# An expert layer that adds its rows to x in memory, in place of a last stage that gathers them

## The reference

```
x = x + m                                   # m: the token mixers
h = rmsnorm(x, norm2_w)
p_grp = softmax(h @ w_router_g)             # 4 groups, the best one is taken
le_sel = (h @ w_router_e) of that group     # 4 experts in it
top_v, top_i = top_k(softmax(le_sel), 2);  top_v /= sum(top_v)
comb = one_hot(expert) * top_v * p_top      # 2 of 16 experts have a weight
act = silu(h @ w_gate[e]) * (h @ w_up[e]) * comb[e]
x = x + sum over e of act @ w_down[e]
y = rmsnorm(x, final_norm_w)
```

## Time and profile before

| | us |
|---|---|
| median of three runs | 1851.73 |
| the profiled execution, of which all rows below are | 1848.95 |
| its span, first to last instruction | 1847.1 |
| expert rounds, first gather wait to last store issue | about 1380 to 1781 |
| final stage, first load of x to the end | 1789.2 to 1847.1 |

### The profile page before, as it was taken

The page is one execution under the profiler, slowest core; times in us unless marked ns, Lnnn a source line. Parts: engine busy times, 40 slices in busy tenths (PEclk is TensorE's granted clock), DMA queues, the critical chain, the costliest instruction groups (busy, mean ns, idle before and its releaser), DMA issues. The chain is left out here.

```text
span 1847.1 us, 24874 instructions
## 1 busy us (share of the span) xinstructions
PE 1468.5 (80%) x8651; PEld 1301.3 (70%) x8651; DVE 1025.1 (55%) x1328; ACT 610.6 (33%) x918; POOL 343.7 (19%) x327
## 2 busy tenths in 40 slices
PE   3789999999997278878876956999928888798940
PEld 2789999999994277777766814888726667577730
DVE  4775455212222466666765146554158887788937
ACT  3332222211103023223322003333216665667723
POOL 0000001000000133242240000000002444344532
PEclk8899999999998589989987557999958998999975
DMA  2111122321112412112112044333146667653238
GB/s 119 53 45 46 35 81 82 113 90 55 65 36 111 136 26 45 30 25 50 25 25 111 1 155 154 119 104 103 49 171 227 231 229 270 251 207 113 92 139 321
DMA packets 91580, 200.53 MB, mean 109 GB/s; under 512 B 39227, under 2 KB 59963, under 8 KB 86655
## 3 DMA queue, kind: packets, MB, share of 16 engines
q1 hardware_dynamic: 74031, 135.48, 22.8%
q0 software_dynamic: 17488, 64.32, 9.6%
HBM read 205.96 MB, written 47.29 MB: 137 GB/s over the span
## 5 line engine op out<-in xcount | busy, mean ns | idle before, releaser
L87 DVE TENSOR_TENSOR c_wlo<-c_w,c_whi 128x1024 fp32r<-128x1024 f32 x40 | 49.0, 1226 | 262.7 <-ACT c_whi L82 262.4
L98 PE MATMUL c_ps<-hn_lo,c_whi 128*128 128x368 f32 x960 | 182.4, 332 | 7.0 <-DVE c_wlo L87 7.0
L98 PE MATMUL c_ps<-hn_hi,c_wlo 128*128 128x368 f32 x960 | 181.3, 331 | 0.0
L98 PE MATMUL c_ps<-hn_hi,c_whi 128*128 128x368 f32 x960 | 181.1, 331 | 0.0
L2244 DVE TENSOR_TENSOR e_winlo<-e_win,e_winhi 128x2048 fp32r<-128x2048 f32 x66 | 153.6, 2330 | 46.8 <-ACT e_winhi L2193 36.9
L98 PEld LDWEIGHTS c_ps<-hn_lo,c_whi 128*128 128x128 f32 x960 | 164.9, 189 | 7.3 <-DVE c_wlo L87 7.3
L98 PEld LDWEIGHTS c_ps<-hn_hi,c_wlo 128*128 128x128 f32 x960 | 164.3, 188 | 0.0
L98 PEld LDWEIGHTS c_ps<-hn_hi,c_whi 128*128 128x128 f32 x960 | 163.9, 188 | 0.0
L2193 ACT CAST e_winhi<-e_win 128x2048 fp32r x66 | 122.5, 1905 | 62.4 <-issue 42.4
L2107 POOL TENSOR_TENSOR e_wdnlo<-e_wdn,e_wdnhi 128x1024 fp32r<-128x1024 f32 x33 | 91.5, 2773 | 234.8 <-ACT e_wdnhi L2201 234.8
L82 ACT CAST c_whi<-c_w 128x1024 fp32r<-128x1024 f32 x40 | 42.1, 1052 | 224.7 <-PE c_ps L98 219.0
(11 more groups left out here) (466 smaller groups left out, 2978.9 us busy)
## 6 DMA issues: line engine op xcount, KB each, us to landing
e_win<-in_w_gate_up SPq DMA_DIRECT2D x33, 2048.0 KB
e_wdn<-in_w_down SPq DMA_DIRECT2D x33, 1024.0 KB
c_w<-in_w_in SPq DMA_DIRECT2D x40, 512.0 KB, 3.6
expert_rows<-e_ys POOLq DMA_DIRECT2D x33, 512.0 KB, 5.5
rc_eb<-g_rows SPq DMA_DIRECT2D x10, 624.0 KB, 5.3
o_land<-in_w_out SPq DMA_DIRECT2D x8, 768.0 KB, 4.9
rc_gb<-g_rows SPq DMA_DIRECT2D x11, 507.0 KB
n_x<-in_xT SPq DMA_DIRECT2D x2, 2208.0 KB, 10.2
```

The costliest lines, as they stand in the source:

```text
L87: return dve.tensor_tensor(dst, src, hi.bitcast(F32), ALU.subtract)
L98: mm = pe.matmul(dst, left(x, k), right(z, k), start=(n == 0 and k == 0), stop=(n == 2 and k == ks - 1))
```

## The change

The expert rows are no longer kept in a tensor of their own. Each round's rows are multiplied by their slot's weight while they are taken from PSUM (`slot_w`, one value for each of the 128 slots of the round), and POOL sends them by an indirect transfer with the operation add to the rows of `x2_dram` that `idx_out` names. An empty slot has the weight 0 and points to one of 128 spare rows behind the 1104, its own lane's; the spare rows are filled once, in the mixer output stage. Since a token has two rows in different rounds, a transfer may not start before the one of the round ahead has landed: POOL waits for `y_sent` of it. The routing stage makes `slot_w` and the occupancy of the slots with the same matmul as `idx_in`, 99 columns wide in place of 33. The last stage has no gathers and no weights: it loads x, takes the norm and stores.

```diff
--- before.py
+++ after.py
@@ -1587,9 +1587,11 @@
                 pool.dma_start(x2_dram[cols(t), :], x2[0:n]).then_inc(x2_sent, 16)
+                if t == 0:
+                    pool.dma_start(x2_dram[T:T + P, :], x2).then_inc(x2_sent, 16)
...
@@ -1906,7 +1909,7 @@
                 for i in range(k * NT9, (k + 1) * NT9):
-                    mm = pe.matmul(ps_idx[:, 0:NBLK], lo_hot[:, i, :], tok_hi[:, i, :], start=(i == 0), stop=(i == NK - 1))
+                    mm = pe.matmul(ps_idx[:, 0:3 * NBLK], lo_hot[:, i, :], tok_hi[:, i].rearrange("p a r -> p (a r)"), start=(i == 0), stop=(i == NK - 1))
...
@@ -2007,16 +2012,20 @@
-            dve.tensor_tensor(tok_hi[:].rearrange("p (k t) r -> p k t r", k=TOPK),
-                              hi_hot[:].rearrange("p (k t) r -> p k t r", k=TOPK),
-                              tok[:].unsqueeze(1).unsqueeze(3).to_broadcast([P, TOPK, NT9, NBLK]), ALU.mult
-                              ).then_inc(ready, 1)
+            per_pair = [tok[:].unsqueeze(1).unsqueeze(3).to_broadcast([P, TOPK, NT9, NBLK]),
+                        wts[:].rearrange("p k t o -> p (k t o)").unsqueeze(2).to_broadcast([P, NK, NBLK]),
+                        valid[:].unsqueeze(1).to_broadcast([P, TOPK, NT9, NBLK])]
+            for i, ap in enumerate(per_pair):
...
+                ins = dve.tensor_tensor(out, hot_, ap, ALU.mult)
+            ins.then_inc(ready, 1)
...
@@ -2024,6 +2033,10 @@
             dve.tensor_copy(idx_in[:], ps_idx[:, 0:NBLK]).then_inc(ready, 1)
+            link(dve.tensor_scalar(unused[:], ps_idx[:, 2 * NBLK:3 * NBLK], -1.0, 1.0, ALU.mult, ALU.add))
+            link(dve.scalar_tensor_tensor(unused[:], unused[:], spare[:], ps_idx[:, 0:NBLK], ALU.mult, ALU.add))
+            dve.tensor_copy(idx_out[:], unused[:])
+            dve.tensor_copy(slot_w[:], ps_idx[:, NBLK:2 * NBLK])
...
@@ -2113,7 +2125,10 @@
                     pool.wait_ge(ys_b, o + 1)
-                    pool.dma_start(y_of[o], ys[:, o % 2, :]).then_inc(y_sent[o % 2], 16)
+                    if o:
+                        pool.wait_ge(y_sent[(o - 1) % 2], 16 * ((o - 1) // 2 + 1))
+                    pool.indirect_dma_start(x2_dram, bass.IndirectOffsetOnAxis(ap=idx_out[:, o:o + 1], axis=0),
+                                            ys[:, o % 2, :], None, compute_op=ALU.add).then_inc(y_sent[o % 2], 16)
@@ -2212,7 +2227,7 @@
-                act.copy(ys[:, r % 2, 0:512], ps_d[:, 0, :]).then_inc(ys_a, 1)
+                act.activation(ys[:, r % 2, 0:512], ps_d[:, 0, :], ACT.Copy, scale=slot_w[:, r:r + 1]).then_inc(ys_a, 1)
@@ -2259,7 +2274,7 @@
-                    dve.tensor_copy(ys[:, o % 2, 512:], ps_d[:, 1, :]).then_inc(ys_b, 1)
+                    dve.tensor_scalar(ys[:, o % 2, 512:], ps_d[:, 1, :], slot_w[:, o:o + 1], None, ALU.mult).then_inc(ys_b, 1)
...
@@ -2302,53 +2315,37 @@
-        @block.gpsimd
-        def _(pool):
...
+        @block.scalar
+        def _(act):
+            act.wait_ge(eps_set, 1)
...
+                act.wait_ge(loaded[t // 3], 48)
+                if t:
+                    act.wait_ge(squared, t)
+                act.activation(junk[0:n], x[0:n, t, :], ACT.Square, accum_out=q[0:n, t, :]).then_inc(squared, 1)
+                act.wait_ge(squared, t + 1)
+                act.activation(q[0:n, t, :], q[0:n, t, :], ACT.Sqrt, scale=1.0 / D, bias=eps[0:n]).then_inc(rooted, 1)
...
+                dve.wait_ge(rooted, t + 1)
+                dve.reciprocal(q[0:n, t, :], q[0:n, t, :]).then_inc(inverted, 1)
+                dve.wait_ge(inverted, t + 1)
+                dve.wait_ge(loaded[t // 3], 48)
+                dve.scalar_tensor_tensor(x[0:n, t, :], x[0:n, t, :], q[0:n, t, :], wf[0:n, :], ALU.mult,
+                                         ALU.mult).then_inc(done, 1)
```

More of the change, by code:

```diff
@@ L1836, in gather, with routing_phase @@
                                        ).then_inc(self.xs_loaded[r % 3], 16)
-def routing_phase(nc, io, ex, lg, wts, idx_in, idx_y, tab, masks, ones, h2_dram):
+def routing_phase(nc, io, ex, lg, slot_w, idx_in, idx_out, tab, masks, ones, h2_dram):
     NT9, NK = NTILE, TOPK * NTILE
@@ L2282, in _, with combine_phase @@
                                       wdn_r[0][:, r % 2, :, 0:512].bitcast(F32), ALU.subtract).then_inc(wdn_lo, 1)
-def combine_phase(nc, io, wts, idx_y, x2_dram, y_dram):
-    BUFS = 4
+def combine_phase(nc, io, x2_dram):
     with ExitStack() as stack:
         m = Memory(nc, stack)
-        wf = m.sb("f_w", [P, D])
-        x = m.sb("f_x", [P, NTILE, D])
-        r1, r2 = m.sb("f_r1", [P, BUFS, D]), m.sb("f_r2", [P, BUFS, D])
+        wf, x = m.sb("f_w", [P, D]), m.sb("f_x", [P, NTILE, D])
         junk, q, eps = m.sb("f_junk", [P, D]), m.sb("f_q", [P, NTILE, 1]), m.sb("f_eps", [P, 1])
-        out_sent, loaded = m.sem("f_sent"), [m.sem(f"f_l{i}") for i in range(3)]
-        gathered = [m.sem(f"f_g{b}") for b in range(BUFS)]
-        added, scaled, rooted = m.sem("f_added"), m.sem("f_scaled"), m.sem("f_rooted")
+        w_loaded, out_sent = m.sem("f_wl"), m.sem("f_sent")
+        loaded = [m.sem(f"f_l{i}") for i in range(3)]
+        eps_set, squared, rooted, inverted, done = (m.sem("f_eps"), m.sem("f_square"), m.sem("f_root"), m.sem("f_inv"),
+                                                    m.sem("f_done"))
         block = stack.enter_context(nc.Block())
@@ L2304, in _ @@
                 if t == 0:
-                    sp.dma_start(wf[:], io["final_row"].partition_broadcast(P)).then_inc(loaded[0], 16)
+                    sp.dma_start(wf[:], io["final_row"].partition_broadcast(P)).then_inc(w_loaded, 16)
             for t in range(NTILE):
                 n = tile_rows(t)
-                sp.wait_ge(scaled, 2 * t + 2)
+                sp.wait_ge(done, t + 1)
                 sp.dma_start(io["y"][t * P:t * P + n, :], x[0:n, t, :]).then_inc(out_sent, 16)
             sp.wait_ge(out_sent, 16 * NTILE)
-        @block.gpsimd
-        def _(pool):
+        @block.scalar
+        def _(act):
+            act.wait_ge(eps_set, 1)
             for t in range(NTILE):
                 n = tile_rows(t)
[L2316 to L2330, removed]
+                act.wait_ge(loaded[t // 3], 48)
[3 more added lines that the diff above has]
+                act.wait_ge(squared, t + 1)
                 act.activation(q[0:n, t, :], q[0:n, t, :], ACT.Sqrt, scale=1.0 / D, bias=eps[0:n]).then_inc(rooted, 1)
@@ L2334, in _ @@
         def _(dve):
[L2335 to L2351, removed]
+            dve.memset(eps[:], EPS).then_inc(eps_set, 1)
+            dve.wait_ge(w_loaded, 16)
+            for t in range(NTILE):
+                n = tile_rows(t)
+                dve.wait_ge(rooted, t + 1)
[4 more added lines that the diff above has]
+                                         ALU.mult).then_inc(done, 1)
 def program(nc, io):
@@ L2388, in program @@
             ex = Experts(Memory(nc, experts))
-            routing_phase(nc, io, ex, lg, wts, idx_in, idx_y, tab, masks, ones, h2_dram)
-            expert_phase(nc, io, ex, idx_in, tab, masks, h2_dram, y_dram)
-        combine_phase(nc, io, wts, idx_y, x2_dram, y_dram)
+            routing_phase(nc, io, ex, lg, slot_w, idx_in, idx_out, tab, masks, ones, h2_dram)
+            expert_phase(nc, io, ex, idx_in, idx_out, slot_w, tab, masks, h2_dram, x2_dram)
+        combine_phase(nc, io, x2_dram)
 def channel_blocks(a):
```

26 lines of the change are left out of this document (15 added, 11 removed).

## The result

| | before | after |
|---|---|---|
| median, us | 1851.62 (4 runs) | 1880.95 (4 runs, 1879.35 to 1888.32) |
| profiled execution / its span | 1848.95 / 1847.1 | 1881.43 / 1879.7 |

The ratio is 1.0165, 95% interval 1.0132 to 1.0199: under 2%, but clear of the noise. The prediction was 1849, with 0.47 for slower and 0.41 for faster; the time is inside its range (1829 to 1893) and on the other side of before than the forecast.

What follows compares the result with a forecast made beforehand. The final stage was taken as bound by transfers, the late expert rounds as paced by DVE. Terms of -30 + 13 + 10 + 4 = -3 us gave 1849 us (chance 0.36), range 1829 to 1893.

Steps and rivals of the forecast that it cites:

- Part 1: Final stage: without gathers and their DVE operations it takes 27.9 us against 57.9, -30 us, paced by ACT.
- Part 2: Accumulate in place of store: lands in 5.75 us alone, 7.0 behind a gather, 10.3 beside weights.
- L: Time from a transfer's issue to its landing; for the accumulate put at 5.75 to 10.3 us.
- Part 3: Expert rounds: quiet ones absorb the later landing, 12 rounds that wait already grow 1.1 us each, +13 us.
- 9.8 + 4.5 + L: e_ys buffer loop: ACT iteration, POOL's path to the issue and the landing must fit in two rounds.
- Up to 11 us it costs nothing: POOL's new wait in the rounds asks for an accumulate issued 11 us earlier, so shorter landings are free.
- Part 4: Tail of the rounds: the last three accumulates wait for one another, 17.25 us against 7.2, +10 us.
- Part 5: Routing: two more DVE products, wider matmuls and four small DVE operations, 3.8 us together, +4 us.
- A: Rival, slower: accumulates land over 2.5 us later than stores, ACT's e_ys wait paces rounds; +48, 1900 us; chance 0.27.
- C: Rival: POOL's accumulate descriptors wait for DVE, 2.86 us in place of 1.0; +20, 1872 us; chance 0.10.
- B: Rival, faster: the extra read is hidden in the queue and rounds lose nothing; -21, 1831 us; chance 0.25.
- Rows landing one after another: Upper bound for the accumulate: each of an engine's 8 rows makes its whole trip before the next, 20 us.

Runs made afterwards that it cites:

- I: The changed kernel with the weight loads inside the rounds cut to 16 elements of each partition: 1827.92 us, ratio 0.9857 to before.
- M: The changed kernel with the 2 MB load of next weights issued only after POOL has written the accumulate's descriptors: 1850.86 us, ratio 0.9995 to before.
- C: The changed kernel with the same indirect transfer overwriting instead of adding: 1854.82 us, ratio 1.0021 to before.
- H: The kernel before the change with a third e_ys buffer and nothing else: 1829.42 us, ratio 0.9875 to before.
- B: The changed kernel with a plain store to a tensor of its own, keeping POOL's wait for the transfer ahead: 1826.98 us, ratio 0.9880 to before.
- G: The changed kernel accumulating to separate rows for each slot, without the wait for the transfer ahead: 1873.11 us, ratio 1.0111 to before.
- K: The kernel before the change with its store first in POOL's round, ahead of subtraction and gather: 1824.50 us, ratio 0.9832 to before.

## Why the prediction was wrong

**Part 1** (-30): right, -29.1, in part because two errors cancel. The first group of loads landed 9.7 us into the stage (8.1 in the sum), and behind it a tile took 1.39 us (1.58 in the sum) and DVE, not ACT, set that pace:

```profile
1852.56 8.09 DMA f_x<-x_rows
...
1860.73 1.15 ACT f_junk L2333 x2
...
1873.54 0.95 DVE f_x L2347
```

**Part 2**: right alone and in quiet rounds, wrong beside weights, where L was put at 10.3 us, the plain store's 8.1 plus the second read. The sum let the transfer's bytes grow in the queue and left its start where it was. But the descriptors are written for 1.6 us, or for 3.2, while the store's took 0.6, and in that time the next load of weights is issued. I shows that the weights make the long landings, M that holding them back shortens most of these, and C that more than half of the growth of the median comes without the add.

**Part 3** (+13) is the step that failed; the rounds cost 49.8 us. Its formula was right: the loop measured 14.7 + L where it says 9.8 + 4.5 + L, and with the measured 13.6 it would have given 14.0 us for a busy round against 14.1. Two things in its use were not. L was put at 10.3 us, where the 11 late ones of the accumulates that ACT waited for took 11.7 to 14.5, 13.6 in the loop above, 3.3 more. And the growth was charged to the 12 rounds that waited already, half of it each, where the loop, once it is the longest, sets all 20 busy rounds: 20 x 1.94 = 39 us. The quiet rounds took no cost in it and lose 9 x 0.97 = 9: with L at 6.9 and the loop's first half at 15.3 to 20.3 us in the four that ACT waited for (1772.0 to 1792.3 is the longest, with 3.4 us for the subtraction and 2.9 for the gather) they are past the slack too. That slack was over-read as well: 10.9 us is not the quiet rounds' own pace, for with a third buffer they take 10.2 (H). And what sets that pace is open; PE is busy in the earlier trace rows as long as DVE, 104.9 and 103.4 us. "Up to 11 us it costs nothing" was right: in the nine busy rounds where the serial wait bit, POOL came to it 8.9 to 11.8 us after the issue ahead, the landings took 11.7 to 14.5, and even so no cost shows (B and G). The forecast of no such wait outside the tail failed because L was too small.

**Part 4** (+10): nearly right, +12.8; three landings of 6.1 to 6.3 us and 0.8 us between a landing and the next issue, which the sum had left out:

```profile
1825.43 1.55 POOL L2130 DMA_INDIRECT x_rows<-e_ys,idx_out  x1 [0.16 <-issue]
1832.26 1.55 POOL L2130 DMA_INDIRECT x_rows<-e_ys,idx_out  x1 [5.28 <-DVE e_ys L2277]
1839.08 1.54 POOL L2130 DMA_INDIRECT x_rows<-e_ys,idx_out  x1 [5.27 <-DMA x_rows<-e_ys,idx_out]
```

**Part 5** (+4): too much. From the first product to idx_in's cast it is 10.8 us where the earlier trace rows have 10.4. The 99-column matmuls took less in all than the 33-column ones did (6.91 us at a granted clock of 0.59, 7.86 at 0.50), so the two products ahead are nearly given back:

```profile
1362.28 6.91 PE L1912 MATMUL r_idx<-r_tokhi,r_lohot 128*128 128x99 f32 x36 [10.49 <-DVE r_lohot L2027]
```

**The rivals** (A to D are those of the prediction here, and not the kernels of the table). A named what happened: ACT's wait for e_ys paces the rounds once the landing grows. It put the time at 1900 with +5 us in every round; the +5 came in about every second busy round and not in the quiet ones. C named the other half, descriptors at 2.86 us: 3.16 or more were measured, in 8 of the 20 busy rounds. Each of the eight began 0.4 to 0.6 us into DVE's subtraction that makes e_winlo, as the one of 1454.75 did:

```profile
1454.16 2.27 DVE L2259 TENSOR_TENSOR e_winlo<-e_win,e_winhi 128x2048 fp32r<-128x2048 f32 x1
```

Where that subtraction began after the accumulate (those of 1568.52 and 1609.77) the writing took 1.6 us, and a plain store that began 0.3 us into it (1455.43 in the kernel with the plain store and the serial wait) took 0.60, like all 20 there. So the accumulate's descriptors suffer like the gathers', as C had it. The section of the Trainium skill cited there ("SBUF — State Buffer", "Who interferes with whom") gives a `tensor_tensor` no two-port mode and lets it contend only with GpSimd's reads; so the rule on two-port operations, as the prediction has it, does not cover these rows, and which port is fought for no run here shows. The sum for C added the longer writing to POOL's time; by kernel M most of the cost lies in how the long writing and the load of weights fall together. B, a faster kernel, would have needed another order or a third buffer. Rows landing one after another, 20 us, did not come: 6.1 us alone. With the rule of the Trainium skill, "DMA: Bandwidth & Descriptors", section "Two DMAs through the same engine are not ordered", that descriptors of a queue are pipelined, the trace agrees as far as these 6.1 us go.

## What to carry to other kernels

When a transfer gets slower to issue or to land, write down the loop of its buffer (fill, wait in the issuing engine's list, descriptors, landing) and compare it with as many rounds as there are buffers; past that point every round pays, here half of each microsecond with two buffers, and not only the rounds that waited before. Look for the cheapest half to cut: here moving the issue ahead of unrelated work on its engine, or more buffers (four in after, three in before), was worth more than the change itself, in both kernels. Two versions should be compared with that wait out of the way, or a change that saves 12 to 17 us measures as one that costs 29.

## What was not expected of the hardware

- How long a transfer's descriptors are being written can decide what it queues behind. With a 2 MB load issued 1.3 to 1.9 us after its start, a plain store (0.60 us to write) mostly landed in 5.1 to 5.9 us and an accumulate (3.16 to 3.33 us) in 12.7 to 14.5. M supports the reading; that it is this order and nothing else was not shown, and two plain stores of K took 8.3 and 9.2 us.
- A 128-row accumulate alone lands 6.1 us from its issue, the same indirect transfer without the add in 3.3, the plain store in 2.9. Writing takes 1.55, 0.95 and 0.55 us. So the add costs more than the indirect addressing, alone 2.8 us against 0.4.
- 36 matmuls of 99 columns took 6.91 us and 36 of 33 columns 7.86: with the granted clock at 0.59 in the one and 0.50 in the other, an estimate for the full clock is 4.1 and 3.9 us (6.91 x 0.59 and 7.86 x 0.50). Three times the columns cost next to nothing here.
